# Attention of a diffusion block on one core: two heads share the halves of TensorE's columns, and the values of all heads are projected together

## The reference

```
kv = (rms_norm(c_kv, kv_norm) @ w_ukv).reshape(..., MLA_HEADS, MLA_NOPE + MLA_V)      # 256 -> 8 x (64 + 64)
k_nope, v = kv[..., :MLA_NOPE], kv[..., MLA_NOPE:]
q = (rms_norm(c_q, q_norm) @ w_uq).reshape(..., MLA_HEADS, MLA_NOPE + MLA_ROPE)       # 384 -> 8 x (64 + 32)
s = jnp.einsum('bqhd,bkhd->bhqk', q, k).astype(jnp.float32) * MLA_SCALE
p = jax.nn.softmax(s, axis=-1).astype(v.dtype)
return jnp.einsum('bhqk,bkhd->bqhd', p, v)
```

## Time and profile before

| | |
|---|---|
| median of 3 runs | 4696.09 us (4693.68 to 4701.34) |
| profiled execution | span 4695.2 us |
| TensorE, VectorE, ScalarE, GpSimd busy | 4141.2, 3229.3, 1554.8, 1466.2 us |
| projections of the stage | 298.75 to 376.30 us |
| steps of the stage | 376.30 to 533.62 us |

### The profile page before, as it was taken

How to read it: one execution, slowest core, us unless ns; L and a number is a source line. 1 busy time by engine, 2 the same in 40 slices (tenths; PEclk the granted TensorE clock), 3 DMA queues, 4 the chain that set the end, 5 groups by cost and what they waited for, 6 DMA issues and landing times. The chain is left out here.

```text
span 4695.2 us, 73645 instructions
## 1 busy us (share of the span) xinstructions
PE 4141.2 (88%) x23812; PEld 2273.5 (48%) x23812; DVE 3229.3 (69%) x10527; ACT 1554.8 (33%) x1960; POOL 1466.2 (31%) x1087
## 2 busy tenths in 40 slices
PE   5999778889999999699999996867898797889996
PEld 1556564556565566344444441433456464534442
DVE  2025544147787797798888875773298898788887
ACT  0014321024444444322222211870154343333332
POOL 0500000321111111266666640211412232277774
PEclk8989989899999999899999997988999998999998
DMA  5100221256877877799999975112488999999996
GB/s 212 57 24 3 74 73 72 86 137 164 238 202 184 239 213 177 242 356 343 347 343 345 343 258 191 56 47 78 141 228 266 318 302 306 297 338 345 345 345 227
DMA packets 374798, 1004.83 MB, mean 214 GB/s; under 512 B 35024, under 2 KB 121872, under 8 KB 367248
## 3 DMA queue, kind: packets, MB, share of 16 engines
q1 hardware_dynamic: 208188, 522.43, 32.4%
q0 software_dynamic: 101376, 318.81, 24.2%
q10 hardware_dynamic: 64996, 160.55, 9.1%
HBM read 804.43 MB, written 146.90 MB: 203 GB/s over the span
## 5 line engine op out<-in xcount | busy, mean ns | idle before, releaser
L1369 PE MATMUL ca_A<-hh,ca_uh 128*128 128x512 f16 (+2 forms) x3072 | 794.8, 313 | 133.1 <-DMA ca_ul<-ca_ur 66.0
L1369 PE MATMUL ca_A<-hl,ca_uh 128*128 128x512 f16 (+2 forms) x3072 | 793.9, 313 | 0.0
L1369 PE MATMUL ca_A<-hh,ca_ul 128*128 128x512 f16 (+2 forms) x3072 | 793.0, 313 | 0.0
L1333 POOL DMA_DIRECT2D ca_ul<-ca_ur x192 | 172.1, 897 | 1145.0 <-ACT ca_ul L1402 1114.1
L1879 PE MATMUL ex_R<-ex_vh,ex_wh 128*128 128x512 f16 x1280 | 486.1, 380 | 29.5 <-DVE ex_wl L1893 29.4
L1879 PE MATMUL ex_R<-ex_vl,ex_wh 128*128 128x512 f16 x1280 | 486.1, 380 | 0.0
L1879 PE MATMUL ex_R<-ex_vh,ex_wl 128*128 128x512 f16 x1280 | 485.9, 380 | 0.0
L1369 PEld LDWEIGHTS ca_A<-hh,ca_uh 128*128 128x128 f16 x3072 | 261.4, 99 | 324.7 <-issue 83.2
L1410 ACT ACTIVATE ca_ga<-ca_A 128x640 f32<-128x640 f32 (+1 forms) x256 | 152.8, 597 | 685.2 <-PE ca_A L1369 626.0
L1369 PEld LDWEIGHTS ca_A<-hh,ca_ul 128*128 128x128 f16 x3072 | 261.6, 99 | 195.3 <-issue 13.1
L1369 PEld LDWEIGHTS ca_A<-hl,ca_uh 128*128 128x128 f16 x3072 | 261.6, 99 | 190.4 <-issue 12.0
(11 more groups left out here) (374 smaller groups left out, 7923.1 us busy)
## 6 DMA issues: line engine op xcount, KB each, us to landing
ca_ur<-in_peer_u SPq DMA_DIRECT2D x256, 512.0 KB, 4.7
ex_vr<-in_peer_v SPq DMA_DIRECT2D x256, 512.0 KB, 7.5
gates<-ca_stage ACTq DMA_DIRECT2D x32, 2048.0 KB, 10.9
ca_ul<-ca_ur POOLq DMA_DIRECT2D x192, 256.0 KB, 5.6
acts<-ca_ga ACTq DMA_DIRECT2D x128, 320.0 KB, 2.5
ex_gr<-gates SPq DMA_DIRECT2D x32, 1280.0 KB, 7.8
ex_ar<-acts SPq DMA_DIRECT2D x128, 320.0 KB, 5.1
acts<-ca_ga ACTq DMA_DIRECT2D x128, 192.0 KB, 5.0
```

The lines of the kernel that those rows point to most:

```text
L1333: nc.gpsimd.dma_start(ul[j][:, :, :].rearrange("p k n -> p (k n)"), ur[j][:, :, :].rearrange("p k n -> p (k n)"), accum_op=ALU.add).then_i ...
L1369: last = nc.tensor.matmul(A[b][:, a:a + w], lhs[j][:, k, :], rhs[:, k, a:a + w], start=(k == 0 and x == 0), stop=(k == KD - 1 and x == 2))
```

## The change

Heads go in pairs (2g, 2g + 1), here called s = 0 and 1.

- The host lays the weights out anew: `ev_w_up` holds a head's query and key weights (256 KB instead of 320 KB), and a new input `ev_w_up_v` holds the value weights of all heads (512 KB), loaded once to `wv`.
- The keys of a pair are made together: `key_pair(g)` writes head s to partitions 64s to 64s + 63 of `T`, and its products alternate between the two. ScalarE copies them out one head at a time, as before.
- The values of all heads come from `values(t)`: for token tile t, 2 products with 512 moving columns, into `C[t % 2]`. Two tiles stand behind each of the first three pairs of heads.
- SP loads the weights of the next pair when the keys of this one are done.
- A step n is now head 2g + s and query tile i, with the two heads of a pair in turn. `mix_values(m)` does the value products of steps 2m and 2m + 1 together, into partitions 0 to 63 and 64 to 127 of `O[m % 2]`, block by block in turn; it stands on TensorE behind the scores of step 2m + 4. `probT` has four buffers (two of them in `rot`), and VectorE copies 128 partitions to `MIX` once in two steps.

```diff
+    PAIRS = HEADS // 2
     STEPS = HEADS * TILES
+    W_Q, W_K = 3 * P, 2 * NOPE
...
+        w = [sb(f"at_w{j}", [P, W_Q + W_K]) for j in range(2)]
+        wv = sb("at_wv", [P, 2, HEADS * V_DIM])
...
+        probT = [sb(f"at_pT{j}", [P, TOK]) for j in range(2)] + [rot[:, j, :] for j in range(2)]
...
-        C = ps("at_C", [P, TILES, V_DIM])
-        O0 = ps("at_O", [P, P])
-        O = (O0[0:64, :], C[0:64, 0:2, :].rearrange("p a d -> p (a d)"))
-        names = ("cs_in", "w_in0", "w_in1", "q_done", "k_done", "v_done", "q_copied", "k_copied", "v_copied", "roped", "score", "maxed",
+        C = [ps(f"at_C{j}", [P, HEADS * V_DIM]) for j in range(2)]
+        O = [x[:, 0:P] for x in C]
...
+            def place(n):
+                m, s = divmod(n, 2)
+                g, i = divmod(m, TILES)
+                return 2 * g + s, i
+
+            keys = lambda n: CTX if place(n)[1] < CTX_TILES else TOK
...
-                    for h in range(1, HEADS):
-                        if h >= 2:
-                            sp.wait_ge(v_done, h - 1)
-                        sp.dma_start(w[h % 2][:, :, :], io["ev_w_up"][h].rearrange("p (k m) -> p k m", k=5)).then_inc(w_in[h % 2], 16)
+                    sp.dma_start(wv[:, :, :], io["ev_w_up_v"]).then_inc(wv_in, 16)
+                    for g in range(1, PAIRS):
+                        sp.wait_ge(k_done, g)
+                        for s in range(2):
+                            sp.dma_start(w[s][:, :], io["ev_w_up"][2 * g + s]).then_inc(w_in[s], 16)
...
+                    def key_pair(g):
+                        if g >= 1:
+                            pe.wait_ge(k_copied, 2 * g)
                         for a, n in HALVES:
                             for kk in range(2):
-                                last = nc.tensor.matmul(T[0:64, a:a + n], w[j][:, 3 + kk, 0:64], PT[:, C_KV + kk, a:a + n],
-                                                        start=(kk == 0), stop=(kk == 1))
+                                for s in range(2):
+                                    last = nc.tensor.matmul(T[64 * s:64 * s + 64, a:a + n], w[s][:, W_Q + kk * NOPE:W_Q + kk * NOPE + NOPE],
+                                                            PT[:, C_KV + kk, a:a + n], start=(kk == 0), stop=(kk == 1))
                         last.then_inc(k_done, 1)
-                        if h >= 1:
-                            pe.wait_ge(v_copied, h)
-                        for t in range(TILES):
-                            for kk in range(2):
-                                last = nc.tensor.matmul(C[:, t, :], PT[:, C_KV + kk, t * P:t * P + P],
-                                                        w[j][:, 3 + kk, 64:128], start=(kk == 0), stop=(kk == 1))
+
+                    def values(t):
+                        if t >= 2:
+                            pe.wait_ge(v_copied, t - 1)
+                        for kk in range(2):
+                            last = nc.tensor.matmul(C[t % 2][:, :], PT[:, C_KV + kk, t * P:t * P + P], wv[:, kk, :],
+                                                    start=(kk == 0), stop=(kk == 1))
                         last.then_inc(v_done, 1)
...
+                    def turn(n):
                         pe.wait_ge(normed, n + 1)
                         if n >= 1:
                             pe.wait_ge(pt_copied, n)
                         for b in range(keys(n) // P):
                             last = nc.tensor.transpose(T[:, b * P:b * P + P], prob[n % 2][:, b * P:b * P + P], ident[:, :])
                         last.then_inc(turned, 1)
+
+                    def mix_values(m):
+                        pe.wait_ge(pt_copied, 2 * m + 2)
+                        if m >= 2:
+                            pe.wait_ge(out_copied, m - 1)
+                        blocks = keys(2 * m) // P
+                        for b in range(blocks):
+                            for s in range(2):
+                                h, i = place(2 * m + s)
+                                last = nc.tensor.matmul(O[m % 2][64 * s:64 * s + 64, :], v[:, h, b, :],
+                                                        probT[(2 * m + s) % 4][:, b * P:b * P + P], start=(b == 0), stop=(b == blocks - 1))
+                        last.then_inc(av_done, 1)
+
+                    for g in range(PAIRS):
+                        queries(2 * g)
+                        queries(2 * g + 1)
+                        key_pair(g)
+                        if g == 0:
+                            pe.wait_ge(wv_in, 16)
+                        for t in range(2 * g, min(2 * g + 2, TILES)):
+                            values(t)
+                    pe.wait_ge(q_copied, HEADS)
+                    pe.wait_ge(k_copied, HEADS)
+                    pe.wait_ge(roped, HEADS)
+                    scores(0)
+                    scores(1)
+                    pe.wait_ge(v_copied, TILES)
+                    for n in range(STEPS):
+                        turn(n)
                         if n + 2 < STEPS:
                             scores(n + 2)
-                        pe.wait_ge(pt_copied, n + 1)
-                        if n >= 2:
-                            pe.wait_ge(out_copied, n - 1)
-                        for b in range(keys(n) // P):
-                            last = nc.tensor.matmul(O[n % 2], v[:, h, b, :], probT[n % 2][:, b * P:b * P + P],
-                                                    start=(b == 0), stop=(b == keys(n) // P - 1))
-                        last.then_inc(av_done, 1)
+                        if n >= 2 and n % 2 == 0:
+                            mix_values(n // 2 - 1)
+                    mix_values(STEPS // 2 - 1)
...
+                    for g in range(PAIRS):
+                        for s in range(2):
+                            h = 2 * g + s
+                            act.wait_ge(q_done, h + 1)
+                            nc.scalar.activation(q[0:64, h, :], A[s][0:64, 0:TOK], ACT.Copy).then_inc(q_copied, 1)
+                        act.wait_ge(k_done, g + 1)
+                        for s in range(2):
+                            nc.scalar.activation(k[2 * g + s][0:64, :], T[64 * s:64 * s + 64, 0:TOK], ACT.Copy).then_inc(k_copied, 1)
+                        for t in range(2 * g, min(2 * g + 2, TILES)):
+                            act.wait_ge(v_done, t + 1)
+                            nc.scalar.activation(v[:, :, t, :], C[t % 2][:, :].rearrange("p (h d) -> p h d", d=V_DIM), ACT.Copy).then_inc(v_copied, 1)
+                    act.wait_ge(roped, HEADS)
...
-                            if o >= 2:
-                                act.wait_ge(av_done, o - 1)
-                            nc.scalar.activation(probT[o % 2][:, 0:keys(o)], T[:, 0:keys(o)], ACT.Copy).then_inc(pt_copied, 1)
+                            if o >= 4:
+                                act.wait_ge(av_done, o // 2 - 1)
+                            nc.scalar.activation(probT[o % 4][:, 0:keys(o)], T[:, 0:keys(o)], ACT.Copy).then_inc(pt_copied, 1)
...
-                        if n >= 2:
-                            o = n - 2
-                            h, i = divmod(o, TILES)
-                            dve.wait_ge(av_done, o + 1)
-                            nc.vector.tensor_copy(MIX[64 * (h % 2):64 * (h % 2) + 64, h // 2, i * P:i * P + P], O[o % 2]).then_inc(out_copied, 1)
+                        if n >= 4 and n % 2 == 0:
+                            m = n // 2 - 2
+                            g, i = divmod(m, TILES)
+                            dve.wait_ge(av_done, m + 1)
+                            nc.vector.tensor_copy(MIX[:, g, i * P:i * P + P], O[m % 2]).then_inc(out_copied, 1)
```

More of the change, by code:

```diff
@@ L372, in attention @@
         cs = sb("at_cs", [P, TOK])
-        w = [sb(f"at_w{j}", [P, 5, P]) for j in range(2)]
+        w = [sb(f"at_w{j}", [P, W_Q + W_K]) for j in range(2)]
+        wv = sb("at_wv", [P, 2, HEADS * V_DIM])
         q = sb("at_q", [96, HEADS, TOK])
@@ L381, in attention @@
         prob = [sb(f"at_p{j}", [P, TOK]) for j in range(2)]
-        probT = [sb(f"at_pT{j}", [P, TOK]) for j in range(2)]
+        probT = [sb(f"at_pT{j}", [P, TOK]) for j in range(2)] + [rot[:, j, :] for j in range(2)]
         small = sb("at_small", [P, 2, 4])
@@ L386, in attention @@
         T = ps("at_T", [P, 1024])
-        C = ps("at_C", [P, TILES, V_DIM])
-        O0 = ps("at_O", [P, P])
-        O = (O0[0:64, :], C[0:64, 0:2, :].rearrange("p a d -> p (a d)"))
-        names = ("cs_in", "w_in0", "w_in1", "q_done", "k_done", "v_done", "q_copied", "k_copied", "v_copied", "roped", "score", "maxed",
+        C = [ps(f"at_C{j}", [P, HEADS * V_DIM]) for j in range(2)]
+        O = [x[:, 0:P] for x in C]
+        names = ("cs_in", "wv_in", "w_in0", "w_in1", "q_done", "k_done", "v_done", "q_copied", "k_copied", "v_copied", "roped", "score", "maxed",
                  "exped", "normed", "turned", "pt_copied", "av_done", "out_copied", "own")
```

(41 more changed lines are left out.)

8 lines of the change are left out of this document (2 added, 6 removed).

## The result

The changed kernel takes 4669.43 us (median of 4 runs, 4666.65 to 4674.7) against 4698.72 (4 runs, 4693.68 to 4702.92) for the kernel before, timed on the same chip: ratio 0.9941, 95% interval 0.9927 to 0.9955. It is 0.6% faster. The forecast was 4646.3 us, in a range of 4636 to 4668: the direction was right, the gain 20 to 23 us too large, and the time lies just above the range.

A forecast was written before the change was run, and what follows sets the result against it. TensorE bounds the stage now, then the VectorE-ScalarE chain. Projections 20.0 us less and steps 29.8 less make 49.8; 4695.2 - 49.8 = 4645.4 us of span, plus 0.9 gives 4646.3 us, range 4636 to 4668.

The forecast's parts named there:

- The step that failed: Whole span: the stage is in series with the rest, so its 49.8 us gain would be the span's.
- my rivals: Halves don't overlap, 4674 us (chance 0.09); chain bunches, 4661 us (0.10); clock falls, 4736 us (0.03).
- the term for "the stages behind": Stages after attention: about 4 us in the range for where the clock's drops fall.
- Halves run beside each other: Key and value products on TensorE: two column halves at once, 16 key records in 2.8 us, 24 value records in 1.5.
- The rule on weight loads: Skill's rule: weight loads overlap matmuls only where row groups differ; would lead to the 4674 us rival, chance 0.09.
- Projections: Query, key and value products ahead of the steps: 57.6 us, 20.0 less.
- The 0.6 us for weight loads: Projections: queries wait for the next pair's weights, 0.2 us three times.
- The 1.85 us of bare copies: End of projections: ScalarE's two key copies of 0.80 us lie bare between last keys and scores, with the ends 1.85.
- The chain becomes the bound: Steps: VectorE and ScalarE's maximum, exp, scaling, next maximum take 2.94 us a long step, 30.3 a pair; TensorE 26.6.
- Steps, mis-sized: The stage's loop of steps: start 1.45, four pairs 122.4, end 3.6 and 0.1, together 127.5 us, 29.8 less.
- the first term, the start: Start of the steps: 3.15 us to the end of the first scaling, not the chain's 1.70, so 1.45 us added.
- The clock as a rival: Steps: idle TensorE drops the whole loop to 1.2 GHz, total 4736 us, 0.85% slower; chance 0.03.

The follow-up runs named there:

- The 32 increments: Changed kernel plus 32 increments of a spare semaphore on TensorE at the start of `attention`, only moving the code behind: 4652.13 us, ratio 0.9901.
- 152 increments: Kernel before, attention untouched, plus 76 + 76 spare-semaphore increments on TensorE, at the start of `attention` and of the stage behind it: 4736.16 us, ratio 1.0087.
- The order experiment: Changed kernel with a pair's key and value products ordered all of one head, then the other, instead of in turn: 4671.79 us, ratio 0.9949.
- Taking the ring apart on both sides: Changed kernel, 32 increments, early exp table load, scores of n + 2 ahead of transposes of n, maximum of n ahead of scaling of n - 1: 4638.04 us.
- the early scores alone: Changed kernel, 32 increments, early exp table load, TensorE making scores of n + 2 ahead of transposes of n: 4646.52 us, ratio 0.9891.
- the early maximum alone: Changed kernel, 32 increments, VectorE taking the maximum of n ahead of the scaling of n - 1: 4715.69 us, ratio 1.0045.

## Why the prediction was wrong

- **The step that failed** is in its first paragraph: "The change touches nothing else... What the stage loses or gains, the span loses or gains." The stage gained 47.0 us, and a loop half a millisecond later, with unchanged code, took 19 away. The 32 increments, which change only the place, won 17.3 of those (4669.43 to 4652.13), and 152 increments brought the same loss to the kernel before. None of my rivals named it; the term for "the stages behind" was nothing in the sum and 4 us in the range.
- **Halves run beside each other**: right. 2.80 and 1.53 us were forecast as 2.8 and 1.5. The order experiment shows that long runs of one half lose part of it (2.45 us) and runs of two products nothing (2.85).
- **The rule on weight loads** (the Trainium skill, "TensorE: Matmul & The Clock Gate", "Part 3: Packing small matmuls — row/col tiling") would have left the value products at 3 us. The measurement decides against it here: 24 weight loads took 1.29 us beside 24 products in 1.53 us, with all 128 rows in common and other columns.
- **Projections**: 57.8 for 57.6 us, so close in part by luck. The 0.6 us for weight loads did not come: all 7.1 us of waiting for them stand before the first product, ahead of this window. But the first two heads' queries took 10.90 us (298.06 to 308.96) and not 5.85 + 4.02, and the wide values 3 x 3.54 = 10.6 and not 10.3. The 1.85 us of bare copies were 1.78.
- **The chain becomes the bound**: right, 2.93 for 2.94 us, 1.70 for short steps, 30.53 for 30.6 us a pair. Taking the ring apart on both sides moved the bound back to TensorE, which shows it; the early scores alone left long steps at 2.93 us, the early maximum alone did harm.
- **Steps, mis-sized**: 130.1 for 127.5 us. It is the first term, the start, put at 1.45 us and measured at 34.70 - 30.6 = 4.1. The 1.45 holds the table load and nothing for the lower clock that follows, which the prediction names only in a rival, as the 3.4 us of the kernel before; it was 10.2 us here, now with the chain as the bound. The pair with 3.4 us more of it took 1.1 us longer, which fits; the clock was not switched off by itself.
- **The clock as a rival**: it did not fall in the loop's later short steps, and stood at 1.00 from 369 us on. It is a real one all the same: with the early maximum, where TensorE waited more, it fell in every pair of heads and the steps had 0.82.

## What to carry to other kernels

An edit that changes how many instructions an engine has ahead of a loop also moves that loop against the blocks in which its instructions come. After such a change compare the gaps at the jumps of every later loop, and try a few dozen empty instructions before blaming the edit. Where a chain over two engines is the bound, find the whole ring first: one order turned alone cost 64 us, part of it by the clock, and both together took 8 us off the steps.

## What the runs showed of the hardware

- At each jump back of this loop TensorE stood still for 1.3 to 5.0 us (three jumps in each of twelve kernels). Where the kernel's place put a second gap two or ten products behind the loop's top, it was 1.0 to 5.6 us and ended 1.25 to 1.58 us after a packet of instructions had landed, with stretches at the lower clock behind it: 19 to 21 us over three jumps, except 10 in the kernel with serial halves.
- Products in two halves of the columns, all rows in common, took the time of one. Written one head after the other, 12 and 12 records, they took 2.45 us instead of 1.53, still below 3.04; by the starts of the records the second head's began three ahead of their turn.
- Empty semaphore increments on TensorE weren't free in front of a wait: 50 put the stage's first product off by 7.8 us and 76 by 9.8. With 32 it stood at 298.74 to 300.29 us in six kernels, with 16 at 298.24, with none at 297.41 to 298.75, so that their cost is not much above the scatter. Why the step between 32 and 50 is so large was not tried.
